# Three-branch attention: a later copy step, query pairs turned one step ahead, and the second query group's rotation in two parts

## What is computed

```python
q, kc, vc, ks, vs, kw, vw, gl = split_cols(u @ w_in, C_WIDTHS)
q = partial_rope_2(q.reshape(b, s, 16, 64), cos, sin)        # likewise kc, ks, kw
kc, vc = compress(k_cmp, pe_k, wk1, wk2), compress(v_cmp, pe_v, wv1, wv2)   # 31 windows
# per block of 128 queries t = 0..3
p_c = masked_softmax(q @ kc * scale, cmp_end <= t); o_c = p_c @ vc
p_s = masked_softmax(q @ k_sel * scale, valid_s);   o_s = p_s @ v_sel
p_w = masked_softmax(q @ k_win * scale, valid_w);   o_w = p_w @ v_win
out = g0 * o_c + g1 * o_s + g2 * o_w                          # sigmoid gates
h = h + out @ w_out;  h = h + sqrelu_mlp(rms_norm(h), w1, w2)
```

## Time and profile before

| | before |
|---|---|
| median of 3 runs | 2239.44 us (2238.37 to 2240.22) |
| profiled execution | 2240.65 us, of which the span 2238.5 us |
| TensorE matmul busy | 2006.6 us (90%) |
| VectorE, ScalarE, GpSimd busy | 746.2, 721.2, 630.3 us |
| third attention, from the last compressed product to its last value product | 1621 to 1820 us of the span |

### The profile page before, as it was taken

The page is one execution under the profiler, slowest core; times in us unless marked ns, Lnnn a source line. Parts: engine busy times, 40 slices in busy tenths (PEclk is TensorE's granted clock), DMA queues, the critical chain, the costliest instruction groups (busy, mean ns, idle before and its releaser), DMA issues.

```text
span 2238.5 us, 27141 instructions
## 1 busy us (share of the span) xinstructions
PE 2006.6 (90%) x10969; PEld 1544.1 (69%) x10969; DVE 746.2 (33%) x1699; ACT 721.2 (32%) x1272; POOL 630.3 (28%) x314
## 2 busy tenths in 40 slices
PE   4999989587785899999889999989969898999998
PEld 3877878522222694466878888879947687888886
DVE  2160343411111525553232222231257633232223
ACT  3223631310001423245242222232156644332222
POOL 1344223000001320000334444432125533444442
PEclk8999999798898897999899999999979999999999
DMA  5323103679997520200113223212310012323220
GB/s 174 113 76 113 39 1 132 252 305 421 422 421 287 167 100 14 74 2 1 59 55 113 88 101 113 76 60 76 68 46 2 1 39 76 107 82 113 76 76 38
DMA packets 82317, 256.23 MB, mean 114 GB/s; under 512 B 10352, under 2 KB 13616, under 8 KB 69904
## 3 DMA queue, kind: packets, MB, share of 16 engines
q1 hardware_dynamic: 70288, 228.14, 27.5%
q0 software_dynamic: 3728, 13.50, 1.7%
q10 hardware_dynamic: 8176, 12.84, 1.5%
HBM read 241.89 MB, written 12.58 MB: 114 GB/s over the span
## 4 chain that ended last, share of the span: by engine, by line
PE 82%; DVE 6%; issue 4%; ACT 4%; DMA 1%; ACTq 1%; POOL 1%; DVEq 0%; SPq 0%; POOLq 0%
PE psA L1207 53%; PE psS L1384 6%; PE psS L1160 4%; PE psA L1107 3%; PE psA L1364 2%; PE psO L1181 2%; PE psA L1084 2%; PE psT L1169 1%; PE psO L1565 1%; PE psA L1094 1%; PE psT L1602 1%; ACTq L1764 1%; PE psA L1468 1%; ACT tok L1635 1%; DVE big L2101 1%
## 5 line engine op out<-in xcount | busy, mean ns | idle before, releaser
L948 POOL TENSOR_TENSOR w_lo<-ring,w_hi 128x2048 fp32r<-128x2048 f32 (+2 forms) x44 | 200.4, 4556 | 558.4 <-ACT w_hi L1635 558.4
L2101 DVE TENSOR_TENSOR x<-psA,x 128x512 f32<-128x512 f32 (+1 forms) x176 | 108.9, 619 | 329.2 <-PE psA L1207 329.0
L1635 ACT ACTIVATE w_hi<-ring 128x2048 fp32r<-128x2048 f32 (+2 forms) x62 | 117.0, 1887 | 241.3 <-PE psA L1207 241.3
L1207 PE MATMUL psA<-hT_hi,w_lo 128*128 128x512 f32 x512 | 181.9, 394 | 4.9 <-DVE hT_lo L2101 4.9
L1207 PE MATMUL psA<-hT_hi,w_hi 128*128 128x512 f32 x512 | 181.0, 392 | 4.9 <-DVE hT_lo L2101 4.9
L1207 PE MATMUL psA<-w_hi,hid_hi 128*128 128x512 f32 x512 | 178.6, 389 | 0.0
L1207 PE MATMUL psA<-w_lo,hid_hi 128*128 128x512 f32 x512 | 178.5, 389 | 0.0
L1635 ACT ACTIVATE big<-psA 128x512 f32<-128x512 f32 (+7 forms) x158 | 69.2, 461 | 300.0 <-PE psA L1207 148.2
L2101 DVE TENSOR_TENSOR scr<-scr 128x512 f32<-128x512 f32 (+2 forms) x69 | 62.2, 904 | 275.5 <-ACT hid_hi L1635 275.4
L1207 PE MATMUL psA<-hT_lo,w_hi 128*128 128x512 f32 x384 | 150.5, 392 | 0.0
L1207 PE MATMUL psA<-w_hi,hid_lo 128*128 128x512 f32 x384 | 149.4, 389 | 0.0
(11 more groups left out here) (308 smaller groups left out, 4562.2 us busy)
## 6 DMA issues: line engine op xcount, KB each, us to landing
ring<-in_mlp_w SPq DMA_DIRECT2D x32, 2048.0 KB, 8.2
ring<-in_w_in SPq DMA_DIRECT2D x8, 2048.0 KB, 7.9
ring<-in_w_gate_e SPq DMA_DIRECT2D x14, 1024.0 KB, 10.9
ring<-in_w_up_e SPq DMA_DIRECT2D x14, 1024.0 KB, 13.6
ring<-in_w_down_e SPq DMA_DIRECT2D x13, 1024.0 KB, 14.0
big<-in_w_down_e SPq DMA_DIRECT2D x12, 1024.0 KB
ring<-in_ab_w_in SPq DMA_DIRECT2D x5, 2048.0 KB, 8.5
y_dram<-big ACTq DMA_DIRECT2D x16, 512.0 KB, 8.2
```

The source lines that it names most:

```text
L948: nc.gpsimd.tensor_tensor(part(w_lo, c), raw_piece(c), part(w_hi, c).bitcast(F32), ALU.subtract)\
L1207: ins = pe.matmul(o, a, b, start=(at == 1), stop=(at == 3 * len(terms)))
L1635: return nc.scalar.activation(o, i, f, **kw)
L2101: return nc.vector.tensor_tensor(o, a, b, op)
```

## The change

Three things are edited, and none of them adds or removes work of the loop:

1. The copies of turned items stand at i = k+8 of ScalarE's and VectorE's loops instead of k+6, and the value products and the block's output at two steps later (`VALUE_LAG` 10 for 8). The turns, the masks and the number of buffers stay.
2. TensorE turns five query pairs ahead of the loop and the other three at steps 0 to 2; ScalarE handles pairs 4 to 7 at steps 0 to 3 instead of 1 to 4. VectorE stays at steps 1 to 4.
3. The rotation of the second query group is cut in two calls of four heads: one right behind the first group's rotation, the other behind the last projection. The count that TensorE waits for becomes 6.

```diff
-TURN_LAG, VALUE_LAG = 5, 8
+TURN_LAG, COPY_LAG, VALUE_LAG = 5, 8, 10
@@ TensorE
-            pe.wait_ge(heads_ready, 5)
+            pe.wait_ge(heads_ready, 6)
@@ TensorE, nsa_attention
-                    if 1 <= i <= 4:
-                        queries(i + 3)
+                    if i < 3:
+                        queries(i + 5)
@@
-            for j in range(4):
+            for j in range(5):
                 queries(j)
@@ ScalarE, nsa_attention
-                    if 1 <= i <= 4:
-                        queries(i + 3)
+                    if i < 4:
+                        queries(i + 4)
@@
-                    k = i - TURN_LAG - 1
+                    k = i - COPY_LAG
@@ VectorE
-            def query_rope(g):
-
-                for t in (NT - 2, NT - 1):
-                    copied(dve, job("nq", NT * (2 * g + 1) + t))
-                dve.wait_ge(heads_ready, 3 + g)
-                rope(tok.rearrange("p t (j g d) -> p t j g d", g=2, d=HD)[:, :, :, g, :], 8, temps, heads_ready)
+            def query_rope(pieces):
+
+                for c in pieces:
+                    for t in (NT - 2, NT - 1):
+                        copied(dve, job("nq", NT * c + t))
+                g, first, count = pieces[0] // 2, 4 * (pieces[0] % 2), 4 * len(pieces)
+                dve.wait_ge(heads_ready, (3, None, 4, 5)[pieces[0]])
+                rope(tok.rearrange("p t (j g d) -> p t j g d", g=2, d=HD)[:, :, first:first + count, g, :], count, temps, heads_ready)
@@
-            query_rope(0)
+            query_rope((0, 1))
+            query_rope((2,))
@@
-            query_rope(1)
+            query_rope((3,))
```

## The result

The changed kernel takes 2279.26 us (median of 4 runs, 2266.24 to 2281.27), the kernel before 2239.78 us in the runs beside it (2238.37 to 2240.22). The ratio is 1.0165, 95% interval 1.0127 to 1.0204. It is slower, as forecast, but by 39.5 us where 16.1 were forecast, and it lies above the range (2267). The profiled execution took 2280.54 us.

The account below looks back on a forecast made before the run. TensorE was taken as close to its own bound in the third attention's loop. Start -2.9, loop +20.5 and last block -1.5 gave +16.1 us, 2239.4 to 2255.5 us; own range 2244 to 2263, wider range 2232 to 2267.

Parts of the forecast that it names:

- The rule: Third attention's loop: TensorE's turn needs a copy from step i-1, before i-3; its lead falls from about three steps to one.
- What to look for: Loop signs: tile 2 blocks 27 to 29 us, TensorE idle ahead of turns 30 or more, stops of 2 at block ends.
- The start: Ahead of the loop: query pairs gain 3.3 us, rotation 0.8, later values take 1.2; first value product 2.9 earlier.
- The rounds of the query pairs: Start of the loop: ScalarE and VectorE overlap; four rounds fall from 14.0 to 10.0 us, gain 3.3.
- The loop: First value product to the last block's, 139.6 us before: longer by 5.0 + 2.2 + 13.3 = 20.5 us.
- 15 groups outside tile 2: Groups inside blocks of other tile widths: 0.15 us more each, 2.2 in all, since TensorE's work fills the time.
- six groups of tile 2, compressed mask included: Inside two tile 2 blocks: one mask more in the chain, 3.6 us, plus 1.4 for compressed masks, 5.0 together.
- seven crossings: Block ends, up to the next block's first value product: 1.7 to 2.1 us more each, 7 x 1.9 = 13.3.
- The rival that had it: Slower still: TensorE's longer stops bring half clock, some 1.7 us at each of seven crossings, 2267 us; chance 0.08.
- The last block: After the loop's last block begins: no masks to wait for, turns already done, some 1.5 of 16.5 us go.
- Faster: Rival: engines no longer stopped run ahead and TensorE's waits go, half 2230 us, all 2223; chance 0.20.
- no change: Rival: crossings cost under 0.5 us each, the loop loses what the start gains, 2240 us; chance 0.13.

Follow-up runs that it names:

- copy_and_values: The kernel before with copies and value products two steps later and the start as it was: 2282.91 us, ratio 1.0163.
- after_probs8: The changed kernel with an eighth buffer for probabilities, copies still two steps later: 2259.67 us, ratio 1.0103 against the kernel before.
- copy7: The changed kernel with copies and value products one step later instead of two: 2238.29 us, ratio 0.9995 against the kernel before.

## Why the prediction was right in kind and wrong in size

**The rule, and which edit decides: right.** "After, it can't be more than about one" step ahead: the timeline above is that, and copies alone carry 37.4 us. What to look for was named and came: idle ahead of turns 41.1 us for "30 us or more", released by copies (25.3 and 13.2) and hardly by GpSimd (2.4); the copies' wait for turns gone and the masks' in its place; a stop of 1.4 to 2.2 us at each crossing, though in four of the seven it was ScalarE's copy, behind `nsa_out_hi`, that ended it. Blocks of tile 2 take 31.03 and 29.82 us for "27 to 29", so already there it was too little.

**The start: right.** Timeline of after, VectorE, the two parts of the last rotation, for the earlier trace rows:

```profile
1602.53 0.90 DVE L2101 TENSOR_TENSOR scr<-tok,const 128x128 f32<-128x128 f32 x4
...
1623.56 0.90 DVE L2101 TENSOR_TENSOR scr<-tok,const 128x128 f32<-128x128 f32 x4
...
1624.49 0.49 DVE L2101 TENSOR_TENSOR tok<-scr 128x128 f32<-128x128 f32 x2
```

Six instructions in 1.42 us (1623.56 to 1624.98), forecast 1.4, and the part put ahead lies where VectorE had been idle. At 0.90 us for four, an operation of 128 elements is 0.23 us, half as many elements for 0.63 of the time of the 256-element ones of the earlier trace rows. The Trainium skill, "VectorE: DVE Perf Modes", section on the TRN2 errata, has a fixed extra latency per instruction; the trace agrees in kind.

The rounds of the query pairs, for the earlier trace rows, all engines; VectorE's and ScalarE's parts now run beside each other:

```profile
1639.08 1.39 DVE L2101 TENSOR_TENSOR nsa_q<-psA,nsa_q 64x512 fp32r<-64x512 f32 x2
...
1639.60 1.20 ACT L1635 ACTIVATE nsa_q<-psA 64x512 fp32r<-64x512 f32 x2
```

VectorE's parts start at 1639.08, 1642.33, 1645.57 and 1647.40: rounds of 3.25, 3.24 and 1.83 us, forecast 3.25, 3.25 and 1.75. The first value product is 2.2 us earlier. This execution was already 0.8 us late at 1621 us, ahead of the edits (the compressed product at 1621.47 for 1620.67), so what the edits gained is 3.0 against 2.9.

**The loop: +40.2 us for +20.5.** Cut at the same value products, the prediction's own terms measure:

| term of the loop | forecast, us | measured, us |
|---|---|---|
| 15 groups outside tile 2 | 2.2 | 14.3 |
| six groups of tile 2, compressed mask included | 5.0 | 8.6 |
| seven crossings | 13.3 | 17.3 |
| clock | nothing | in the three above, 6 to 14 by estimate |

The steps that failed are two.

*The groups outside tile 2 were put at 0.15 us each, "because TensorE's own work fills the time".* It doesn't fill it. The third group of the first block of tile 1 ran at full clock in both kernels, so nothing but the order differs; before and after:

```profile
1686.23:1690.45 4.22, 3.92 (x36) 3.18 (x35) 3.84 (x17) 3.79 (x13) 2.60 (x5) 1.00 0.01 2
1694.10:1699.17 5.07, 4.12 (x37) 3.41 (x36) 3.37 (x13) 3.25 (x10) 2.62 (x4) 1.00 0.01 2
```

That is 0.85 us, and TensorE is idle for 0.95 of its 5.07. The second group of that block is 4.64 for 3.56, the third of tile 0 4.08 (copy_and_values at full clock) for 3.26. Only the groups of tile 3 come near the forecast, 0.3 us each at full clock. The chain of tile 2 was walked too short as well: the mask starts 0.75 behind its turn and not 0.53, the second mask 0.59 behind the copy and not 0.47, the last turn 0.71 behind ScalarE's copy and not 0.61. I had taken these from the earlier trace rows, where the items are 384 columns wide, for a chain whose items are 512 wide. The crossings are 2.2 to 2.9 us each for 1.9. The walk of tile 2 holds (2.2 for 2.1); with smaller tiles I had 1.7 to 2.1 and the four behind tiles 0 and 1 took 2.2, 2.3, 2.9 and 2.9, the last two at 0.90 of the clock.

*The clock was left out.* The rival that had it stood at 0.08, against it "four windows stayed at 1.00 with such idles in them". That reads the clock from a kernel in which TensorE's idles ahead of turns are short (1.1 us the longest, 13.6 us in all) and carries it over to one in which they are three times as much in all (2.2 us the longest, 41.1 in all). After the change six of seven windows are below 1.00. The rival had the clock at 12 us (7 x 1.7), which lies within the 6 to 14 of the estimates; that it was a rival and not a term is one reason why the time left the range, and the groups are the other. The Trainium skill, "TensorE: Matmul & The Clock Gate", says where it tells of the second failure mode that frequent short idles between groups of matmuls can make the clock swing, and the traces here agree: 0.98 granted over the loop with 13.6 us of idle ahead of turns, 0.88 with 41.1. It is not the sum of the idle alone, though. after_probs8 has 35.6 us of it and 0.97.

**The last block: -1.5 forecast, +0.8 measured.** The turns behind its first value product do help: at full clock copy_and_values, in the same order, takes 14.60 us from its first value product to its last, 0.9 less than the 15.46 before. After ran it at 0.89 and took 16.2.

**The other rivals.** Faster needed a crossing at no cost, no change one below 0.5 us; the crossings cost 2.2 to 2.9 us each more. The query pairs did overlap.

**What stays open.** How much of the 39.5 us the clock is: the estimates say 6 to 14, and no run holds the clock up through the whole loop with the stops in place. Which sign ahead of time would have told that the clock falls isn't known either. Whether the median's 39.5 holds the same share as the profiled execution is open too, since the runs of after lie 15 us apart.

## What to carry to other kernels

Between engines that work through fixed lists, write down for each wait in which step of the other's list its releaser stands, and follow the round until it closes: through every resource, the scores as much as the buffers. Here, with two steps between, moving the copies cost next to nothing (copy7: 2.8 us of loop); at one step the lists closed into one chain and each step cost the sum of its links (38.7 us more, the clock's share in it). A wait that an engine with slack no longer has is no gain, and if TensorE gets stops in exchange, its clock belongs in the sum as a term, also where the kernel before shows it at full.

## What the runs showed of the hardware that I had not expected

- With TensorE's idle ahead of turns up from 13.6 to 41.1 us, half clock in the loop rose from some 6 to 43 us. For 14.8 us on end the clock granted was 0.50 while TensorE was busy for 13.3 of them: at that level, the engine looked nearly full.
- More matmuls did not bring the clock up: with the scores of tile 0 made three times, TensorE was busy for 22.5 of the 22.5 us ahead of the first value product, and the clock granted was 0.50 throughout. Without the added scores it was busy for 10.9 of the last 12.3 us ahead of that product, and 0.78 was granted.
- Runs of one kernel differ with their clock: 2266.24 us at 0.943, 2277.97 at 0.934, 2280.54 at 0.932, 2281.27 at 0.931. The kernel before spread over 1.9 us in the four runs beside it, but over 17 us in a batch of 23, again with the clock (2227.57 us at 0.948, 2244.78 at 0.938).
- A mask that waits for a turn starts 0.15 us behind the end of the turn (1725.97 to 1726.12), where a copy that waits for one starts 0.03 us behind it (1719.26 to 1719.29 in the kernel before). I had taken the copy's link for the mask's.
